# Sixteen decay products and eight total copies move from VectorE to GpSimd

## The reference

```
def rwkv7_features(...):
    ...
    kk = kk * lax.rsqrt(jnp.sum(kk * kk, axis=-1, keepdims=True) + EPS)
    decay = jnp.exp(-jnp.exp(-jax.nn.softplus(-w_log) - 0.5))
    a = jax.nn.sigmoid((a0 + ...).astype(jnp.float32))
    k_dir = k[:, :, None, :].astype(jnp.float32) * (1.0 + (a - 1.0) * k_a)

def step(S, inp):
    r, w, k, v, kk, a = inp
    S = (S * w[:, :, None, :]
         - jnp.einsum('bhvk,bhk->bhv', S, kk)[..., None] * (kk * a)[:, :, None, :]
         + v[..., None] * k[:, :, None, :])
    return S, jnp.einsum('bhvk,bhk->bhv', S, r)
```

## Time and profile before

| | |
|---|---|
| median of 3 runs | 2845.96 us (2841.99 to 2849.18) |
| profiled execution | 2853.77 us, of which the span of the trace is 2851.9 us |
| PE busy | 2590.0 us, 91% |
| DVE busy | 1514.8 us, 53% |
| ACT busy | 893.7 us, 31% |
| POOL busy | 76.7 us, 3% |
| decay stage | about 1170.0 to 1234.8 us of the span |
| mean granted TensorE clock | 0.949 of full speed |

### The profile page before, as it was taken

One profiled execution on the slowest core, in us unless ns is written; L12 is line 12 of the kernel. 1 busy time (PEld: TensorE's weight loads), 2 busy tenths in 40 slices (PEclk: granted clock), 3 DMA queues, 4 the chain that ended last, 5 costly groups with the idle time before them and its releaser, 6 DMA issues.

```text
span 2851.9 us, 41831 instructions
## 1 busy us (share of the span) xinstructions
PE 2590.0 (91%) x17518; PEld 2060.3 (72%) x17518; DVE 1514.8 (53%) x2517; ACT 893.7 (31%) x1547; POOL 76.7 (3%) x148
## 2 busy tenths in 40 slices
PE   8999999899997898469996899998999997888998
PEld 6687778588875666269993588876788875656998
DVE  5656474655554655664444455554555543564554
ACT  2331231422223333612211322222422223343543
POOL 0000000000000000000000000000000000000000
PEclk9999999999998999669998999999999998999999
DMA  7235435344343110000002244343344442101453
GB/s 285 80 116 203 179 120 208 103 143 143 127 160 108 59 45 30 0 2 4 4 4 74 75 147 140 134 154 133 111 148 137 140 144 73 47 30 45 168 188 133
DMA packets 55770, 309.72 MB, mean 109 GB/s; under 512 B 5920, under 2 KB 9376, under 8 KB 28064
## 3 DMA queue, kind: packets, MB, share of 16 engines
q1 hardware_dynamic: 32944, 224.74, 22.1%
q0 software_dynamic: 20736, 75.51, 8.0%
q10 hardware_dynamic: 1904, 6.80, 0.6%
HBM read 305.98 MB, written 1.05 MB: 108 GB/s over the span
## 4 chain that ended last, share of the span: by engine, by line
PE 38%; PEld 33%; issue 11%; DVE 11%; ACT 6%; DMA 1%; PEldq 0%; DVEq 0%; ACTq 0%
PEld bank L1195 11%; PEld bank L1202 11%; PEld bank L1198 10%; PE bank L1075 4%; PE bank L1254 4%; PE bank L1072 2%; PE bank L1048 2%; PE bank L1134 2%; PE bank L1150 2%; PE bank L939 2%; PE bank L1195 2%; PE bank L1198 2%; PE bank L1202 2%; PE bank L946 2%; PE bank L942 2%
## 5 line engine op out<-in xcount | busy, mean ns | idle before, releaser
L1946 DVE TENSOR_TENSOR w_lo<-ring,w_hi 128x1024 fp32r<-128x1024 f32 (+1 forms) x198 | 236.2, 1193 | 450.7 <-ACT w_hi L1488 450.6
L1198 PE MATMUL bank<-ffn_x_lo,w_hi 128*128 128x512 f32 x1008 | 399.6, 396 | 0.0
L1202 PE MATMUL bank<-ffn_x_hi,w_lo 128*128 128x512 f32 x1008 | 399.6, 396 | 0.0
L1195 PE MATMUL bank<-ffn_x_hi,w_hi 128*128 128x512 f32 x1008 | 399.6, 396 | 0.0
L1488 ACT ACTIVATE w_hi<-ring 128x1024 fp32r<-128x1024 f32 (+1 forms) x198 | 203.7, 1029 | 290.2 <-PE bank L1198 278.6
L1878 DVE SCALAR_TENSOR_TENSOR ms<-mod_rows,c_silu 128x1024 f32<-128x1024 f32 x200 | 243.8, 1219 | 1.2
L1202 PEld LDWEIGHTS bank<-ffn_x_hi,w_lo 128*128 128x128 f32 x1008 | 189.9, 188 | 46.3
L1195 PEld LDWEIGHTS bank<-ffn_x_hi,w_hi 128*128 128x128 f32 x1008 | 189.9, 188 | 46.3
L1198 PEld LDWEIGHTS bank<-ffn_x_lo,w_hi 128*128 128x128 f32 x1008 | 189.8, 188 | 46.3
L1195 PE MATMUL bank<-ffn_h_hi,w_hi 128*128 128x512 f32 x528 | 211.7, 401 | 0.0
L1202 PE MATMUL bank<-ffn_h_hi,w_lo 128*128 128x512 f32 x528 | 209.3, 396 | 0.0
(11 more groups left out here) (430 smaller groups left out, 4619.9 us busy)
## 6 DMA issues: line engine op xcount, KB each, us to landing
ring<-in_stream SPq DMA_DIRECT2D x211, 1024.0 KB, 4.8
mod_rows<-in_mod_stream POOLq DMA_DIRECT2D x144, 512.0 KB, 3.8
one_const<-in_one ACTq DMA_DIRECT2D x1, 1665.0 KB, 13.9
mix_const<-in_two ACTq DMA_DIRECT2D x1, 1440.0 KB, 6.3
win_const<-in_win ACTq DMA_DIRECT2D x1, 1089.0 KB, 4.9
x<-in_x SPq DMA_DIRECT2D x4, 256.0 KB, 4.8
c_silu<-in_c SPq DMA_DIRECT2D x1, 1024.0 KB, 9.6
x<-in_x SPq DMA_DIRECT2D x1, 1024.0 KB, 25.8
```

Of the source, the lines that this page charges most:

```text
L1195: mm = pe.matmul(bank[:, 0:tok], w_high, hi, start=k == 0, stop=False)
L1198: mm = pe.matmul(bank[:, 0:tok], w_high, lo, start=False, stop=False)
L1202: mm = pe.matmul(bank[:, 0:tok], w_low, hi, start=False, stop=last)
L1946: V.tensor_tensor(low[:, 0:h.nk, :], raw_half(h), high[:, 0:h.nk, :].bitcast(F32), ALU.subtract).then_inc(sem("w_split"), 1)
```

## The change

GpSimd gets a function `decayed` which runs once, ahead of transfer 78. For each of the eight (`d`, `m`) it waits for `decays_ready`, copies the chunk totals, waits for that copy (`totals`), forms `inc` times r, waits for `rates_scaled`, and forms `exc` times kk. VectorE loses the copy and the two products of each turn and gains a `nop` that signals `rates_scaled` behind `a` times kk. TensorE and VectorE both wait for all eight `shared_products` at the start of `wkv`, which stands behind the barrier.

```
@@ gpsimd
+            def decayed():
+
+                for d in range(2):
+                    for m in range(4):
+                        r, kk = ph3["r"][:, m, :], ph3["kk"][:, m, :]
+                        inc, exc = (ph3["rt"][:, m, :], ph3["kt"][:, m, :]) if d == 0 else (inc1[m], exc1[m])
+                        pool.wait_ge(sem("decays_ready"), 4 * d + m + 1)
+                        last = (C - 1, 0)[d]
+                        nc.gpsimd.tensor_copy(ph3["total"][:, d, m, :], inc.rearrange("p (c t) -> p c t", t=C)[:, :, last]).then_inc(sem("totals"), 1)
+                        pool.wait_ge(sem("totals"), 4 * d + m + 1)
+                        nc.gpsimd.tensor_tensor(inc if d == 0 else r, inc, r, ALU.mult)
+                        pool.wait_ge(sem("rates_scaled"), 4 * d + m + 1)
+                        nc.gpsimd.tensor_tensor(exc if d == 0 else kk, exc, kk, ALU.mult).then_inc(sem("shared_products"), 1)
+
             pool.wait_ge(sem("x_in3"), 16)
             for n in range(2 * 2 * MOD_TILES):
                 if n >= 2:
                     pool.wait_ge(sem("mod_rows_used"), n - 1)
-                if n in (2 * MOD_AFTER_SCAN, 2 * MOD_AFTER_SCAN + 1):
+                if n == 2 * MOD_AFTER_SCAN:
+                    decayed()
                     pool.wait_ge(sem("scan_done"), 3)
@@ tensor
             def wkv():
+                pe.wait_ge(sem("shared_products"), 8)
@@ vector, decays, d = 0
-                    V.tensor_copy(ph3["total"][:, 0, m, :], chunks(inc)[:, :, C - 1])
                     link(V.tensor_scalar(lw, a, -1.0, param("k_a", m), ALU.add, ALU.mult))
-                    V.tensor_tensor(inc, inc, ph3["r"][:, m, :], ALU.mult)
                     link(V.scalar_tensor_tensor(lw, lw, 1.0, ph3["k"][:, m, :], ALU.add, ALU.mult))
-                    V.tensor_tensor(exc, exc, ph3["kk"][:, m, :], ALU.mult)
                     link(V.tensor_tensor(a, a, ph3["kk"][:, m, :], ALU.mult))
+                    dve.nop().then_inc(sem("rates_scaled"), 1)
                     link(V.tensor_tensor(lw, lw, bt, ALU.mult))
                     link(V.tensor_tensor(bt, bt, a, ALU.mult))
@@ vector, decays, d = 1: the same three removed (r, kk) and the same nop added
@@ vector
             def wkv():
+                dve.wait_ge(sem("shared_products"), 8)
```

More of the change, by code:

```diff
@@ L2310, in decays @@
                 for m in range(4):
-                    lw, inc, exc, bt, a = ph3["lw"][:, m, :], ph3["rt"][:, m, :], ph3["kt"][:, m, :], ph3["bt"][:, m, :], rates[0][m]
+                    lw, bt, a = ph3["lw"][:, m, :], ph3["bt"][:, m, :], rates[0][m]
                     dve.wait_ge(sem("decays_ready"), m + 1)
-                    V.tensor_copy(ph3["total"][:, 0, m, :], chunks(inc)[:, :, C - 1])
                     link(V.tensor_scalar(lw, a, -1.0, param("k_a", m), ALU.add, ALU.mult))
-                    V.tensor_tensor(inc, inc, ph3["r"][:, m, :], ALU.mult)
                     link(V.scalar_tensor_tensor(lw, lw, 1.0, ph3["k"][:, m, :], ALU.add, ALU.mult))
-                    V.tensor_tensor(exc, exc, ph3["kk"][:, m, :], ALU.mult)
                     link(V.tensor_tensor(a, a, ph3["kk"][:, m, :], ALU.mult))
+                    dve.nop().then_inc(sem("rates_scaled"), 1)
                     link(V.tensor_tensor(lw, lw, bt, ALU.mult))
@@ L2321, in decays @@
                 for m in range(4):
-                    r, k, kk, bt = (scan[1][n][:, m, :] for n in ("rt", "lw", "kt", "bt"))
-                    step, inc, exc, a = sig1[m], inc1[m], exc1[m], rates[1][m]
+                    k, kk, bt = (scan[1][n][:, m, :] for n in ("lw", "kt", "bt"))
+                    step, a = sig1[m], rates[1][m]
                     dve.wait_ge(sem("decays_ready"), 4 + m + 1)
-                    V.tensor_copy(ph3["total"][:, 1, m, :], chunks(inc)[:, :, 0])
                     link(V.tensor_scalar(step, a, -1.0, param("k_a", m), ALU.add, ALU.mult))
-                    V.tensor_tensor(r, inc, r, ALU.mult)
                     link(V.scalar_tensor_tensor(k, step, 1.0, k, ALU.add, ALU.mult))
                     link(V.tensor_tensor(a, a, kk, ALU.mult))
-                    V.tensor_tensor(kk, exc, kk, ALU.mult)
+                    dve.nop().then_inc(sem("rates_scaled"), 1)
                     link(V.tensor_tensor(k, k, bt, ALU.mult))
```

## The result

| | changed kernel | kernel before, same chip | ratio (95% interval) |
|---|---|---|---|
| first comparison, 7 and 7 runs | 2861.07 us (2856.15 to 2867.7) | 2846.4 us (2841.99 to 2854.14) | 1.0034 (1.0020 to 1.0048) |
| second comparison, 12 and 23 runs | 2855.03 us (2845.74 to 2864.01) | 2851.12 us (2842.12 to 2856.74) | 1.0020 (1.0005 to 1.0036) |

What follows compares the result with a forecast made beforehand. VectorE's second part was taken as the only chain in its stage; −10.3 + 1.0 + 19.5 + 1.4 − 1.8 = +9.8 us gave 2855.8 us (+0.34%) against the 2845.96 median, range 2835 to 2866.

Steps and rivals of the forecast that it cites:

- What bounds the stage: VectorE's second part, 1197.10 to 1234.80: VectorE is the only chain there, while TensorE and ScalarE wait for its barrier.
- The saving, 10.3 us: VectorE's eight turns: removing the copy (0.08 us) and two products (0.60 and 0.61) saves 1.29 us a turn.
- the nops, 1.0 us: VectorE's eight turns: the nop signalling rates_scaled between two linked products adds 0.12 us each.
- The price of a GpSimd product, 1.22 us: Each 128x512 product on GpSimd, priced like VectorE's scan, bounds 0.69 and 2.45; sixteen are 19.5 us.
- In turns: VectorE's second part: GpSimd and VectorE alternate at the memory, so GpSimd's work is added to the chain; +9.8 us, chance 0.56.
- half-and-half rival: VectorE's second part: the engines share, half of GpSimd's 20.9 us of reading stretches the chain; +1.0 us, 2847 us, chance 0.12.
- The sum of the turns: VectorE's chain: −10.3 removed, +1.0 nops, +19.5 products, +1.4 copies, −1.8 for gaps covered; +9.8 us.
- cover: VectorE's second part: a GpSimd product slipping between two linked VectorE instructions hides 0.11 us of pitch, 16 times, −1.8 us.
- The reload, 5 us within 1.3 to 10: GpSimd's library reload between its first copy and first product, taken as 5 us, costing nothing in the case of turns.
- GpSimd last: Rival: GpSimd's 22.3 us stand nearly alone behind VectorE's end at 1225.3; +12.8 us at most, 2858 us, chance 0.10.
- Each microsecond arrives in full at the end: Behind VectorE's barrier: every microsecond its second part loses or gains reaches the kernel's end, since everything after is dated from it.
- nothing for the clock: Start of the scan: TensorE's granted clock, 0.50 after idling, stays at the same level whatever the stage's length, so 0 us.

Runs made afterwards that it cites:

- e5: Changed kernel with GpSimd starting its eight turns only after VectorE has finished its eighth; 2863.95 us against 2853.28 for the kernel before, ratio 1.0045.
- d1: Kernel before with 138 idle TensorE matmuls while it waits for VectorE's barrier, which lasted longer than VectorE; ratio 1.0113.
- d2: Changed kernel with 167 idle TensorE matmuls while it waits for VectorE's barrier, which lasted longer than VectorE; ratio 1.0193.
- d3: c3 with 121 idle TensorE matmuls while it waits for VectorE's barrier, which outlasted VectorE by 36.3 us; ratio 1.0055.
- e2: Changed kernel with GpSimd's sixteen products replaced by memsets that write zeros and read nothing; 2838.55 us against 2853.28 for the kernel before, ratio 0.9952.
- e3: Changed kernel with GpSimd's sixteen products replaced by copies of 128x512 zeros, one input read instead of two; one execution, 2848.0 us.
- e4: Changed kernel with the eight copies of chunk totals back on VectorE, the products still on GpSimd; 2849.57 us against 2853.28 for the kernel before, ratio 1.0003.
- c2: Kernel before with nine idle linked VectorE products behind the eighth turn, 6.5 us more chain, GpSimd idle; 2853.84 us against 2851.12, ratio 1.0008.
- c3: Kernel before with one VectorE step moved to ScalarE and VectorE's instructions reordered to wait only for the one before the last; 2830.95 us against 2851.12, ratio 0.9948.

## Why the prediction was right, and where its steps were not

**What bounds the stage.** Right. VectorE is the only chain in its second part in all kernels but e5, d1, d2 and d3, where something was put behind it on purpose or by miscount. The 33.1 us of ScalarE are a wait for TensorE's first transposes, which stand behind the barrier, and not one for VectorE itself.

**The saving, 10.3 us, and the nops, 1.0 us.** Right. Without disturbance (e2) the turn is 3.54 us against 4.70 before, and the forecast had 3.53. The pitch across the `nop` is 0.84 us in e2 (1206.49 to 1207.33), against 0.72 without one: 0.12, as taken from the first part.

**The price of a GpSimd product, 1.22 us.** Right: the pitches in e5 are 1.22 and 1.20 us. Chosen as the nearest row within 0.69 and 2.45, it was the scan's, with no better reason than that. By the quarter of the Trainium skill's figure ("GPSIMD Engine Reference", Performance versus the Vector engine), 1.12, the estimate would have been 8% low, and by its ratio, 1.35, 11% high.

**In turns.** Right, and e2 and e3 show it: the memsets did not disturb the two-input instructions beside them, the products and 128x512 copies did, and the hold is for whole instructions, but for 0.14 us. The rule of the Trainium skill ("SBUF — State Buffer", Who interferes with whom) is borne out in the stronger form that I had doubted: a two-input VectorE instruction and a GpSimd instruction that reads exclude each other, while one that only writes does not. e2 and the row of 1.80 us agree with it. The half-and-half rival falls: if the two had shared at a reduced rate, GpSimd's product would be longer, too, but L815 lasts 1.26 us beside a held VectorE and 1.25 to 1.26 alone in e5; and a VectorE slowed in proportion would not come out at the same 0.14 us from an overlap of 0.58 and of 1.25 us. The reason that I gave was too narrow, however. I took the price to go with two inputs, and the tensor_scalar, which reads one tensor, for the exception; yet seven of the eight products with r held the tensor_scalar, at 0.89 us each, 6.2 of the 16.2 us.

**The sum of the turns.** Forecast +9.8 us, measured +6.8: 5.7 in the second part (43.4 against 37.7) and 1.1 in the first, on the held scan. The terms: −10.3, +1.0, and 16 holds that replace products and cover. Eight products with kk held 1.11 each and eight with r seven times 0.89 and once 1.11 (the scan), in all 16.2. I had 19.5 − 1.8 = 17.7 for these, so the cover was mis-sized: it is 3.3 us, 0.21 for each product and not 0.11. The 1.4 us for the copies should not have been in the sum: alone they last 0.19 us each, but they cost the chain nothing (e4), and 3.53 + 1.11 + 0.89 is the whole turn of 5.53 us, where I had 5.9. These two terms are the 3 us by which the sum was too high.

**The reload, 5 us within 1.3 to 10.** Wrong in size and without consequence, as forecast: the gap in which it lies is 0.09 us. The Trainium skill ("GPSIMD Engine Reference", Instruction dispatch) has some 6 us for a first call; no run here shows it. Why it is not seen was not tried.

**GpSimd last.** The sum was 12.8 us for the stage against the kernel before; e5 measured 12.4 (77.2 against 64.8).

**Each microsecond arrives in full at the end; nothing for the clock.** This is the step that failed, in both places. VectorE's chain is 6.8 us longer and the decay stage only 4.3: the granted clock before VectorE's second part was 0.80 instead of 0.66, the stage's first matmuls were busy for 12.4 instead of 17.5 us, and VectorE began its second part 1.4 us sooner, counted from the stage's first matmul. And the scan stage, the same instructions, is 262.4 and 255.5 us instead of 267. I had argued that TensorE's clock is at 0.50 at the barrier in any case and concluded that it costs the same in any case; the traces show that how long it stays there afterwards differs. A mean of 0.62 in 30 us is 22.8 us at half speed, one of 0.87 is 7.8 us. In the profiled pair the scan stage gave back 4.5 us, more than the 4.3 that the decay stage lost, and the span is 2.6 us longer only because the rest of it was 2.8 us longer. By the ratios the change costs 9.7 and 5.7 us (0.34 and 0.20%), both above the 4.3 us of its decay stage, so the times do not show that the scan gives something back, as it did in the profiled pair. In the experiments the end follows the decay stage only roughly: 7.8 us more there and 0.9 in time (e4), 6.5 and 2.3 (c2), 9.5 less and 13.7 less (e2), 10.1 less and 14.8 less (c3), 12.4 more and 12.8 (e5), where each ratio is uncertain by 4 to 6 us. The forecast of 9.8 us meets the first ratio and lies near the upper end of the second's interval, with a chain that cost 3 us less than its sum: the agreement is in part luck.

## What to carry to other kernels

Before work goes from a busy VectorE to an idle GpSimd, look at what both read: a product on GpSimd that reads tensors stops VectorE's two-input instructions, and in this kernel the tensor_scalar as well, until it is all but done. At 0.89 to 1.11 us of hold for 0.60 us saved the move loses, although the other engine stood at 3% of the span. The loss shows as longer durations and not as waits, so compare the mean duration of each line between the two traces. What helped in its place was work for ScalarE, and an order in which no instruction waits for the one directly ahead of it.

## What the runs showed of the hardware that I had not expected

- A GpSimd copy that reads only one tensor (0.61 us, 128x512) also holds a two-input VectorE product, by 0.44 us, and a tensor_scalar by 0.22 us. A product holds a scan as well (2.33 us instead of 1.23). A memset of 0.53 us beside a two-input product holds nothing.
- A signalling `nop` between linked instructions costs 0.12 us, while waiting for the instruction before the last costs nothing that can be seen: a pitch of 0.60 us against 0.72.
- The reload of GpSimd's library took no visible time: 0.09 us from the first copy's end to the first product's start, where other turns have 0.07 to 0.09.
- The same 6976 matmuls of the scan stage took 252.7 to 267.3 us, with a mean granted clock of 0.98 to 0.91. Keeping TensorE busy ahead of them put the low stretch off by 10 us and did not remove it (263.6 us).
